# A mixer and expert layer: experts taken in a fixed pattern of their ranks by size, and the low parts of all expert weights made on VectorE

## The reference, cut to what matters

```python
s = sigmoid(x @ w_router)                  # 64 experts, 8 groups
# 4 groups, then 6 experts of each token; gates are normed and scaled by 2.5
# tokens of each expert are gathered in blocks of 128 (MOE_BLOCK)
def run_block(tok, gw, e):
    return swiglu(x[tok], w1[e], w3[e], w2[e]) * gw[:, None]
routed = segment_sum(y, tok)               # added up by token
out = x + g2 * (routed + swiglu(x, ws1, ws3, ws2))   # a shared expert for all tokens
```

## Time and profile before

| | |
|---|---|
| median of the runs | 2855.18 us |
| profiled execution | 2856.53 us |
| its span, first to last instruction | 2854.9 us |
| mean granted TensorE clock | 0.955 |
| TensorE busy | 2541.4 us, 89% |
| VectorE busy | 1692.9 us, 59% |
| POOL busy | 1364.5 us, 48% |
| ScalarE busy | 1014.7 us, 36% |
| moved by DMA | 641.42 MB, mean 225 GB/s |

### The profile page before, as it was taken

How to read it: one execution, slowest core, us unless ns; L and a number is a source line. 1 busy time by engine, 2 the same in 40 slices (tenths; PEclk the granted TensorE clock), 3 DMA queues, 4 the chain that set the end, 5 groups by cost and what they waited for, 6 DMA issues and landing times. The chain is left out here.

```text
span 2854.9 us, 52119 instructions
## 1 busy us (share of the span) xinstructions
PE 2541.4 (89%) x11953; PEld 2029.2 (71%) x11954; DVE 1692.9 (59%) x2579; ACT 1014.7 (36%) x1615; POOL 1364.5 (48%) x1136
## 2 busy tenths in 40 slices
PE   7999999999849899589999999999998999989991
PEld 4787777777638777478777777777776788767780
DVE  4664554574236777554855575675588644686643
ACT  3212433323212222212543353443356422453422
POOL 1210025612245666421655665665577644576644
PEclk9999999999969999699999999999999999999995
DMA  7775768574456554445986887987799866698747
GB/s 274 305 259 203 265 214 309 196 276 166 163 209 232 170 202 159 149 111 139 340 258 162 248 274 191 271 268 190 200 282 351 285 168 155 183 317 259 209 105 270
DMA packets 247800, 641.42 MB, mean 225 GB/s; under 512 B 32876, under 2 KB 46512, under 8 KB 232240
## 3 DMA queue, kind: packets, MB, share of 16 engines
q1 hardware_dynamic: 188736, 459.72, 44.8%
q0 software_dynamic: 58992, 180.78, 25.9%
HBM read 463.08 MB, written 177.33 MB: 224 GB/s over the span
## 5 line engine op out<-in xcount | busy, mean ns | idle before, releaser
L2154 DVE TENSOR_TENSOR w_exp_lo<-w_exp,w_exp_hi (+1 forms) x256 | 401.8, 1604 | 74.5 <-ACT w_exp_hi L2093 65.5
L2093 ACT ACTIVATE w_exp_hi<-w_exp (+1 forms) x256 | 260.9, 1056 | 220.4 <-issue 130.5
L2280 PE MATMUL ps_h<-w_exp_hi,x_exp_t_hi 128*128 (+1 forms) x1216 | 312.6, 399 | 26.1 <-ACT w_exp_hi L2093 20.3
L2010 POOL TENSOR_TENSOR w_exp_lo<-w_exp,w_exp_hi (+1 forms) x130 | 321.9, 2500 | 13.2 <-ACT w_exp_hi L2097 10.1
L2280 PE MATMUL ps_h<-w_exp_lo,x_exp_t_hi 128*128 (+1 forms) x1216 | 311.6, 398 | 16.9 <-DVE w_exp_lo L2154 16.9
L2280 PE MATMUL ps_h<-w_exp_hi,x_exp_t_lo 128*128 (+1 forms) x1216 | 321.6, 407 | 0.0
L2280 PEld LDWEIGHTS ps_h<-w_exp_hi,x_exp_t_hi 128*128 128x128 f32 x1216 | 228.1, 189 | 88.9 <-ACT w_exp_hi L2093 20.5
L2070 POOL DMA_INDIRECT sum_d<-w_shared_raw,give x136 | 246.1, 1810 | 91.1 <-DVE w_shared_raw L2192 42.9
L2280 PEld LDWEIGHTS ps_h<-w_exp_lo,x_exp_t_hi 128*128 128x128 f32 x1216 | 228.4, 189 | 77.2 <-issue 22.6
L1134 PE MATMUL ps_p<-wa_hi,hx_split 128*128 128x512 f32 x1088 | 279.1, 403 | 4.1 <-DVE kvqg_out L100 3.2
L2060 POOL DMA_DIRECT2D give<-list_d x136 | 76.7, 564 | 399.2 <-issue 391.6
(11 more groups left out here) (270 smaller groups left out, 4390.6 us busy)
## 6 DMA issues: line engine op xcount, KB each, us to landing
w_exp<-in_experts SPq DMA_DIRECT2D x386, 512.0 KB, 7.6
hx_split<-hx_d SPq DMA_DIRECT2D x54, 1024.0 KB, 5.7
rec_m<-rec_d SPq DMA_DIRECT2D x16, 1536.0 KB, 8.8
hx_d<-hx_split SPq DMA_DIRECT2D x18, 1024.0 KB, 5.5
wm_rest<-in_w_mod_rest POOLq DMA_DIRECT2D x16, 1024.0 KB, 5.9
rec_d<-kvqg_out SPq DMA_DIRECT2D x48, 256.0 KB, 4.4
xt<-in_xt POOLq DMA_DIRECT2D x18, 512.0 KB, 8.8
rec_d<-kt_kvf_out SPq DMA_DIRECT2D x32, 256.0 KB, 5.4
```

The lines of the kernel that those rows point to most:

```text
L2010: pool.tensor_tensor(w[1][:, piece(e, i)].bitcast(F32R), raw(e, i), w[0][:, piece(e, i)], ALU.subtract).then_inc(wd_lo, 1)
L2093: act.activation(w[0][:, piece(e, i)].bitcast(F32R), raw(e, i), ACT.Copy).then_inc(gu_hi, 1)
L2154: dve.tensor_tensor(w[1][:, piece(e, i)].bitcast(F32R), raw(e, i), w[0][:, piece(e, i)], ALU.subtract).then_inc(gu_lo, 1)
L2280: last = pe.matmul(out, x[:, j * P:(j + 1) * P].bitcast(F32R), w_part[:, bass.ds(w_at + j * stride, 512)].bitcast(F32R), start=(start and ...
```

## The change

Three things change. The order of experts: VectorE computes for each expert its number of blocks and a key, ranks the experts by it, and a product with a constant matrix brings sizes and numbers into positions; position p takes the expert of rank `bit-reversed p` (`rank_at`), so that larger and smaller ones alternate. SP reads the number of the expert at a position from `ends_row`. The first routed expert is thus known only when the table is there: its load moves behind load 11 of the shared rows and its splits from step 0 to step 12. The low parts of the down weights move from POOL to the end of VectorE's step. And in VectorE's step `weigh` moves one step later, behind the first two splits, and the third split goes behind h's low part.

```diff
+    out["rank_at"] = np.repeat(np.array([[int(f"{p:06b}"[::-1], 2) for p in range(64)]], np.float32), P, 0)
+    FIRST_SPLIT = NT - 4
...
-                return expert_of(eng, k) + 1, k in (0, NT)
+                return expert_of(eng, k) + 1, k in (FIRST_SPLIT, NT)
...
+            def expert_at(e):
+                return sp.value_load(ends_row[0:1, bass.ds(e, 1)], min_val=0, max_val=NE - 1)
...
             def load_free(e, slot):
+                row = expert_at(e)
...
-            for i in range(N_GU + N_D):
-                load(1, 1, i)
             for k in range(STAGES, NT):
                 sp.wait_ge(xt_lo, (k - STAGES + 1) * 2)
                 load_shared(k)
+                if k == 11:
+                    table(sp)
+                    row = expert_at(1)
+                    for i in range(N_GU + N_D):
+                        load(row, 1, i)
...
@@ POOL
-            for i in range(N_GU, N_GU + N_D):
-                split(0, i)
...
-            for i in range(N_GU, N_GU + N_D):
-                split(1, i)
...
-                if before is not None:
-                    at_change(pool, before, split, range(N_GU, N_GU + N_D))
...
@@ VectorE
+            def split_d(e, i):
+                dve.wait_ge(wd_hi, e * N_D + i - N_GU + 1)
+                dve.tensor_tensor(w[1][:, piece(e, i)].bitcast(F32R), raw(e, i), w[0][:, piece(e, i)],
+                                  ALU.subtract).then_inc(wd_lo, 1)
...
                 here = change(dve, k)
-                at_change(dve, here, split, range(3))
+                before = change(dve, k - 1) if not isinstance(k, int) or k > 0 else None
+                at_change(dve, here, split, range(2))
+                if not isinstance(k, int) or k > 1:
+                    weigh(k - 2, par, None if isinstance(k, int) else r - 1)
                 if not isinstance(k, int) or k > 0:
                     copy_ht(k - 1, 1 - par)
+                at_change(dve, here, split, range(2, 3))
...
                 at_change(dve, here, split, range(3, N_GU))
                 if not isinstance(k, int) or k > 0:
-                    weigh(k - 1, 1 - par, None if r is None or (isinstance(k, int) and k == NT) else r - (1 - par))
+                    wait(dve, d_done, k - 1)
+                    at_change(dve, before, split_d, range(N_GU, N_GU + N_D))
...
+                tabs.of(dve.scalar_tensor_tensor(key[:], nt[:, 1:NE], float(N_EXP), R.iota[:], ALU.mult, ALU.subtract))
...
+                tabs.of(dve.tensor_scalar(own_key[:], key[:], kc[:], None, ALU.is_gt))
+                tabs.of(dve.tensor_reduce(rnk[:], own_key[:], AX.X, ALU.add))
+                dve.tensor_scalar(by_size[:, 0], R.rank_at[:], rnk[:], ncol[:], ALU.is_equal, ALU.mult).then_inc(sized, 1)
+                dve.tensor_scalar(by_size[:, 1], R.rank_at[:], rnk[:], R.kcol[:, 2:3], ALU.is_equal, ALU.mult).then_inc(sized, 1)
...
                 if k == 2:
-                    tabs.append(counts())
-                if k == 3:
-                    columns(tabs[0])
+                    sizes(tabs)
+                if k == 4:
+                    counts(tabs)
                 if k == 5:
+                    columns(tabs)
+                if k == 7:
...
@@ TensorE
+                if k == 3:
+                    pe.wait_ge(sized, 2)
+                    pe.matmul(ps_r[:, 0:2 * N_EXP], R.order[:, 1], by_size[:].rearrange("p a e -> p (a e)"),
```

More of the change, by code:

```diff
@@ L1202, in __init__ @@
         self.iota = sb("iota_s", [P, N_EXP])
-        self.kcol = sb("kcol_s", [P, 2])
+        self.kcol = sb("kcol_s", [P, 3])
+        self.rank_at = sb("rank_at_s", [P, N_EXP])
         self.token = sb("token_s", [P, NT], U32)
@@ L1395, in mixer_out @@
         rows_loaded = dma_sem("m_rows_loaded")
-        N_CONST, N_ROWS = 10, 3
+        N_CONST, N_ROWS = 11, 3
         clear(nc, semaphores + R.semaphores())
@@ L1816, in constants @@
     out["list_base"] = (out["iota"] + 1) * 2048
-    out["kcol"] = np.stack([i, i + P], 1).astype(np.float32)
+    out["kcol"] = np.stack([i, i + P, i + 1], 1).astype(np.float32)
+    out["rank_at"] = np.repeat(np.array([[int(f"{p:06b}"[::-1], 2) for p in range(64)]], np.float32), P, 0)
     out["token"] = (np.arange(16)[None] * P + np.arange(P)[:, None]).astype(np.uint32)
@@ L1864, in experts @@
         cmpn = sb("cmp_nt", [P, 2, NE])
+        key = sb("size_key", [P, N_EXP])
+        own_key = sb("size_key_own", [P, N_EXP])
+        kc = sb("size_key_col", [P, 1])
+        ncol = sb("nt_col", [P, 1])
+        rnk = sb("size_rank", [P, 1])
+        by_size = sb("by_size", [P, 2, N_EXP])
+        er = sb("expert_row", [P, NE + 1])
+        de = sb("expert_steps", [P, NE])
+        cmpe = sb("cmp_expert", [P, 2, NE])
+        ecol = sb("expert_cols", [P, 2])
         bcol = sb("block_cols", [P, 2, 2])
@@ L1882, in experts @@
         tab_own, bcol_done, brow_done, rows_done = sem("tab_own"), sem("bcol_done"), sem("brow_done"), sem("rows_done")
+        sized, ordered = sem("sized"), sem("ordered")
         N_ROWS_DONE = 4
@@ L1971, in load_free @@
             def load_free(e, slot):
+                row = expert_at(e)
                 for i in range(N_GU):
                     sp.wait_ge(gu_lo, (e - RING) * N_GU + i + 1)
-                    load(e, slot, i)
+                    load(row, slot, i)
                 for i in range(N_D):
                     sp.wait_ge(wd_lo, (e - RING) * N_D + i + 1)
-                    load(e, slot, N_GU + i)
+                    load(row, slot, N_GU + i)
             for k in range(2):
@@ L1989, in _ @@
                 load_shared(k)
+                if k == 11:
[3 more added lines that the diff above has]
+                        load(row, 1, i)
+            row = expert_at(2)
             sp.wait_ge(xt_lo, NT * 2)
             for i in range(N_GU):
-                load(2, 0, i)
+                load(row, 0, i)
             sp.wait_ge(wd_lo, N_D)
             for i in range(N_GU, N_GU + N_D):
-                load(2, 0, i)
+                load(row, 0, i)
             load_free(3, 1)
@@ L2006, in _ @@
             pool.memset(ones[:], 1.0).then_inc(rows_done, 1)
-            def split(e, i):
-                pool.wait_ge(wd_hi, e * N_D + i - N_GU + 1)
-                pool.tensor_tensor(w[1][:, piece(e, i)].bitcast(F32R), raw(e, i), w[0][:, piece(e, i)],
-                                   ALU.subtract).then_inc(wd_lo, 1)
-            for i in range(N_GU, N_GU + N_D):
-                split(0, i)
             def add(k):
@@ L2022, in _ @@
             enlist(pool, R, NT - 2, 0, list_d)
-            for i in range(N_GU, N_GU + N_D):
-                split(1, i)
             add(0)
             enlist(pool, R, NT - 1, 1, list_d)
-            for k in range(1, 4):
+            for k in range(1, 6):
                 add(k)
@@ L2049, in _ @@
             load_take(NT + 2, 0, 1)
-            for k in range(4, NT - 1):
+            for k in range(6, NT - 1):
                 add(k)
             def step(k, par, r):
-                before = change(pool, k - 1) if not isinstance(k, int) or k > NT else None
                 gather(k + 2, par, r + 1)
                 load_take(k + 3, 1 - par, r + 1 + par)
-                if before is not None:
-                    at_change(pool, before, split, range(N_GU, N_GU + N_D))
                 wait(pool, added, (k - 1) * 16)
@@ L2210, in step, with sizes @@
                 if not isinstance(k, int) or k > 0:
-                    weigh(k - 1, 1 - par, None if r is None or (isinstance(k, int) and k == NT) else r - (1 - par))
-            def counts():
-                tabs = Count(dve, tab_own)
+                    wait(dve, d_done, k - 1)
+                    at_change(dve, before, split_d, range(N_GU, N_GU + N_D))
+            def sizes(tabs):
                 dve.wait_ge(R.carry_done, NT)
@@ L2261, in _ @@
                 split(0, i)
+            for i in range(N_GU, N_GU + N_D):
+                split_d(0, i)
             n = iterations(dve, step, after)
+            weigh(n * 2 + (NT - 2), 0, n - 1)
             copy_ht(n * 2 + (NT - 1), 1)
@@ L2329, in after @@
                     rank(pe, R, NT - 1, ps_r)
-                if k == 4:
+                if k == 3:
+                    pe.wait_ge(sized, 2)
+                    pe.wait_ge(R.carry_done, NT)
+                    pe.matmul(ps_r[:, 0:2 * N_EXP], R.order[:, 1], by_size[:].rearrange("p a e -> p (a e)"),
+                              start=True, stop=True).then_inc(ordered, 1)
+                if k == 6:
                     pe.wait_ge(bcol_done, 2)
-                    pe.wait_ge(R.carry_done, NT)
                     for c in range(2):
```

22 lines of the change are left out of this document (17 added, 5 removed).

## The result

The changed kernel takes 2915.43 us, median of 4 runs (2908.72 to 2919.48), beside 2857.73 for the kernel before on the same chip (4 runs, 2844.31 to 2860.29): ratio 1.0209, 95% interval 1.0171 to 1.0248. It is slower, clear of the interval, by about 2%; a gain of 50 us was forecast. The profiled execution spans 2906.6 us, 51.7 more than before. Of all runs in this document one is left out of its ratio as disturbed: the fourth of e10, 8285.89 us.

What follows compares the result with a forecast made beforehand. The chain of scatters, not TensorE, was taken to pace the routed stage: 1114 + 262 - 25 + 5 + 20 = 1376 us against 1422, -46; start -5; so 2856.5 - 51 = 2805 us, range 2760 to 2848.

Steps and rivals of the forecast that it cites:

- idle time of the chain: Routed blocks: the scatter chain's waits for VectorE's products, 46 us, cut to 20 by the new expert order.
- -25, +5 for the issues: Routed blocks: `give` freed from POOL's splits gains 25 us; scatter issues slowed beside added VectorE pieces cost 5.
- most of the delay is hidden: Weighing one step later, behind two splits: mostly covered by the chain's lag; uncovered, up to 2.45 us a change.
- The waiting: Routed blocks: scatter intervals less scatter-to-`give` time and less 0.9 us; the prediction worked with 46 us, cut to 20.
- rival D: Routed blocks: late weighing costs the chain 2.45 us at each of 62 changes, 152 us; 2940 to 2957; chance 0.07.
- The prediction's own bound: Routed blocks: a scatter may start 7.3 us into TensorE's step, or 3 to 4 where queues are full.
- The 4 us by which the scatter trails the products: Routed blocks under load: the chain starts 4 us behind the products, taken as cover for the later weighing.
- The traffic term: Routed blocks: scatter-to-`give` time over 7.35 us, summed over all pairs; 262 us, or 4.2 a change.
- Start of the stage: Step 0: POOL's splits and expert 1's low parts leave VectorE ahead of the routed blocks; gain 5 us, bounds 0 and 7.8.
- Runs of changes: Routed blocks: six runs of four consecutive expert changes each cost TensorE 3.3 us, 20 in all; runs of two cost nothing.
- rival B: Routed blocks: traffic spreads well and the chain drops below TensorE, 1334 instead of 1422 us; 2763 total; chance 0.27.
- Rival C: Routed blocks: VectorE's new order gives half back, 31 changes losing 1.2 us by later weighing; 2842 total; chance 0.16.

Runs made afterwards that it cites:

- e10: The e1 kernel with the third split again ahead of h's low part; ratio 1.0129, first to last scatter 1465 us.
- e14: The kernel before with only the third split moved behind h's low part; ratio 0.9998, first to last scatter 1428 us.
- e4: The e1 kernel with the low parts of the two down pieces given back to POOL; ratio 0.9980, first to last scatter 1419 us.
- e13: Repeat of e1: the changed kernel with weighing back at the end of VectorE's step, ahead of the down pieces; ratio 0.9865, first to last scatter 1392 us.
- e11: The changed kernel with three splits ahead of the weighing in place of two; ratio 1.0227, first to last scatter 1498 us.
- e5: The kernel before with all low parts on VectorE, down pieces behind the weighing; ratio 1.0168, first to last scatter 1480 us.
- e12: The changed kernel run again unedited in another set; ratio 1.0189, first to last scatter 1484 us.
- e3: The changed kernel with experts in order of their numbers instead of the pattern; ratio 1.0165, first to last scatter 1476 us.
- e9: The e1 kernel with half of each weight piece not moved from expert 3 on; 2803.18 us in one run, beside 2884.89 before.
- e6: The e1 kernel with POOL issuing the scatter ahead of the load of `give`; ratio 1.0145, first to last scatter 1467 us.
- e1: The changed kernel with weighing back at the end of VectorE's step, ahead of the two down pieces; ratio 0.9885, first to last scatter 1390 us.

## Why the prediction was wrong

The kernels before, e14, e4, e13 and the changed one form a ladder, one part of the change at each step:

| step | from | to | the stage | forecast for it |
|---|---|---|---|---|
| third split behind h's low part | before | e14 | 1422 to 1428 | nothing by itself |
| pattern and its tables | e14 | e4 | 1428 to 1419 | -26, idle time of the chain 46 to 20 |
| down pieces to VectorE | e4 | e13 | 1419 to 1392 | -25, +5 for the issues |
| weighing a step later, behind two splits | e13 | changed | 1392 to 1483 | nothing, "most of the delay is hidden" |

**The failed step is the last.** The prediction put it so: "The chain already starts 4 us behind the products under load, so most of the delay is hidden". The waiting rises from 45 to 173 us between e13 and the changed kernel, 128 us or 2.1 a change, near the full 2.45 that rival D charged and twice the 1.05 from which D said it decides. Two things were wrong in it.

The delay was too small. The prediction let the weighing end 2.0 us later in a change step (3.9 instead of 1.9), and up to 7.5 us into a step in a long run. Measured from the end of the down products it ends 4.2 us later in the median of all 136 blocks (5.8 for 1.5), and in the 31 blocks with no split right before it still 2.6 later. Not counted were VectorE's table reads, which now stand directly ahead of the weighing or of the splits before it, and their doubling. The prediction's own bound, that a scatter may start at 3 to 4 us where the queues are full, is passed in the example (5.5 us), and TensorE waits for 61 gathers.

The cover was not there. The 4 us by which the scatter trails the products contain the weighing itself, 1.5 us to its end, and the shortest time from a weighing to its scatter, 0.8. From the end of a weighing to its scatter it is 2.5 us in the median before, so the reserve was 1.7; for 38 of 136 scatters that time was under 1 us and there was none. In the changed kernel it is under 1 us for 101 of them. And a chain that is late because of the traffic has no reserve at a change in any case: what is added to one scatter starts the later ones later, until the next wait takes it up.

D's 152 us were too many as a net price. The traffic term is 34 us lower than in e13; that a chain which is held up leaves the queues emptier is the likely reason, and e11 goes the same way (75 us more waiting, 61 less traffic). The rest of the difference is the gain of the other parts.

**The clock was not in the sum.** The prediction priced a stall by its length. Behind the stall of 2.15 us above lie 1.8 us more. The windows over the stage tell how much that is between e13 and the changed kernel: TensorE is busy 1317.22 us of 1393 in e13 and 1353.73 of 1494 in the changed kernel, so 36 of the 101 us are the same work done more slowly.

```profile
1353.00:2746.00 1393.00, 1317.22 (x6199) 1049.58 (x6197) 939.34 (x1319) 602.08 (x915) 558.24 (x541) 0.99 0.82 240
```

**What was right.** POOL without its splits and VectorE with them: -20 forecast net, -27 measured; the traffic term alone fell by 46 and the waiting rose by 17. This holds with the third split behind h's low part only: with it ahead, e5 loses 58 us. The issues of scatters: +5 forecast, +7 measured. Their median hardly moves (1669 to 1681 ns), but their mean goes from 1810 ns on the page to the 1861 shown above, times 136. The trace shows where it comes from: no issue without a split of VectorE beside it takes over 1.69 us, before or after; with 0.3 us or more of a split beside it the mean is 2.06 us (51 issues) before and 2.16 (53) after, and in e11, whose splits hardly meet a scatter (3 issues), all 136 take 1.69 at most. The prediction had weighed up to 150 us here by the shared port of the Trainium skill (SBUF — State Buffer, section "SBUF: two separate sides"). That section is narrower than the prediction took it: it has descriptors blocked while VectorE is in a 2-port mode, and an instruction with two inputs in SBUF, as a split is, locks out only a GpSimd instruction that reads SBUF. The trace agrees that a split can hold an issue up, by about 1 us at most (2.67 for 1.67), and shows a small price, since few issues meet one.

Start of the stage: 10 us, 5 forecast, beyond the bound of 7.8. TensorE's wait of 7.78 is 2.2 now, near the 2.5 forecast. But from the transposes of block 0 to those of block 16 it is 151.8 us before and 146.5 after (149.4 in e12), so 5.3 of the 10 us lie inside the stage's first steps; the other 4.5 lie ahead of block 0's transposes, and their cause was not tried. Steps 8 to 11, where the table and the load of the first expert were priced at zero, take 37.0 us instead of 34.5.

Runs of changes: laid out by the prediction's list, the six runs of four changes end at blocks 55, 70, 85, 103, 119 and 136; e13 has six steps of over 12 us, at 49, 55, 70, 85, 119 and 136. The forecast was 3.3 us for each; step 85 of e13 (the transposes of h from 2067.20 to 2081.57) is 4.9 us too long, 3.3 forecast; its TensorE rows:

```profile
2067.20 0.38 PE L2332 MATMUL ps_ht<-ident,h_gated 128*128 128x128 f32 x2
...
2073.60 1.22 PE L2323 MATMUL ps_y<-w_exp_hi,h_exp_t_hi 128*128 x2 [3.28 <-DVE h_exp_t_lo L2184]
...
2081.57 0.38 PE L2332 MATMUL ps_ht<-ident,h_gated 128*128 128x128 f32 x2
```

The stall of 3.28 is what was worked out. The rest, 1.6 us, is the slow products behind it: pairs start 0.86 us apart up to 2076.32.

**What was wrong but small.** POOL's splits were held for most of TensorE's wait for h's low part: it went only from 49.0 to 38.6 us with them gone, and to 19.7 in e14, which keeps them and moves the third split alone. The pattern was to halve the chain's idle time; between e14 and e4 the waiting falls by 12 us, and in e3 the stage is even 7 us shorter without it. The traffic per change stays where it was (275 to 278), so rival B, in which it spreads, has nothing for it; even with half the weights (e9) the stage takes 1350 us, more than B's 1334. Rival C had the right mechanism with 1.2 us at half the changes, 37 us, under a third of the 128.

## What to carry over

Work on an engine that feeds the pacing chain is to be put ahead of work that can wait. Before an edit moves it, list everything that will stand between its input and its start, the engine's own register and table reads included, and measure the reserve from the end of that work to its reader, not from an earlier point: here 1.7 us, not 4. A wait's name in the profile is a guess from what landed last; where the named transfer belongs to another block, look at the sequencer's rows (`DVEq`). Price a stall of TensorE with the slow products behind it, not by its length alone. And a move that is free in one kernel (the third split, 6 us) can be worth 73 us in the next, so parts are to be measured in the order in which they are combined.

## What the runs showed of the hardware

- A 1 KB load issued by POOL right behind an indirect scatter lands 6.0 us after its issue in the median (e6), the same load ahead of the scatter after 4.8 (e1) and 2.0 (changed).
- Behind a stall of TensorE of 2.15 us products ran at the 1.2 GHz level for about 3 us (granted clock 0.50 from 2117.2 to 2119.7) and then at 2.4 GHz again. Of 25 stalls of 2 us or more in that stage, 16 were followed by such a stretch. What decides it was not tried.
- VectorE's 128x1024 subtraction takes 1.21 to 1.23 us in the changed kernel, in which POOL has no such instruction, and up to 5.77 beside one. Beside POOL's DMA issues it is not lengthened (197 of them, 1.23 at most), but the issue is: an indirect scatter takes 1.69 us at most alone and 2.06 to 2.16 in the mean beside a split.
- A table entry read from SBUF by VectorE's sequencer takes 0.31 us in the median, at times 1.0 to 1.7, and about 0.6 with the register work around it. In the changed kernel 72 weighings began 0.2 to 0.4 us after such reads had ended, with all that they needed there 1.1 us or more before.
